# A last residual added by an identity product, and weight splits handed out two granules earlier, in a hybrid mLSTM and attention block

## The chip, the cores and the metric

The kernel runs on one NeuronCore of one Trainium2 chip. The metric is the device time of one execution in microseconds. The engines are TensorE (PE, with its weight loads shown as PEld), VectorE (DVE), ScalarE (ACT), GpSimd (POOL) and SyncE (SP, which issues the DMAs of weights and output). Each works through its own list of instructions in order and waits at semaphores for the others.

## The reference

The input x has 512 rows (tokens) of 1024 numbers, all in float32. One layer is computed:

- h = rmsnorm(x); one projection of h gives the inputs of two branches (mLSTM in chunks, forgetting attention) and two gates gm and gf of 1024 channels each.
- mix = sigmoid(gm) * (y_m @ w_br_mlstm) + sigmoid(gf) * (y_f @ w_br_fox), and x = x + mix @ w_out.
- x = x + (silu(h2 @ w_gate) * (h2 @ w_up)) @ w_down, with h2 = rmsnorm(x) and 2816 inner channels.
- The output is rmsnorm(x) with the gain norm_f_g: x * (mean(x * x) + 1e-6) ** -0.5 * gain, row by row.

The change touches two places: the gates gm and gf with the branch projections (the branch stage), and the last residual addition with the final norm (the tail).

## The kernel before

**Products in split float32.** To keep float32 accuracy each operand is held as a high part, rounded to fp32r, and a low part, the rest. One product is then three fp32r products on PE (`three`: high by high, high by low, low by high). Weights come from HBM in slots of 128x2048 numbers into two staging buffers. Each slot holds granules; for each granule ScalarE writes the high part (`split_hi`, L584), VectorE subtracts it from the staged weights for the low part (`split_lo`, L943). A ring of four buffers holds split granules. Semaphores: `hi_split`, `lo_split` and `used` count the granules split high, split low and worked through by PE. SyncE loads a slot when `lo_split` says that the slot two before it is done.

**The branch stage.** It has four rounds c = 0 to 3, two blocks of 128 output channels in each. The round's granules begin at `br_first` = 29, 35, 41 and 51. In rounds 0 and 1 they are four granules of gate weights and two of branch weights (33, 34 and 39, 40). In rounds 2 and 3 each pair of gate blocks is computed by a run of seven products in place of eight: `seven_slot` makes four granules of them (41 to 44 and 45 to 48 in round 2), two of which (42 and 43, the combos) are sums of weight quarters that VectorE computes first in `weight_sums` (L1337 to L1342, four instructions). The results are put together by VectorE's `run_sums` (L1299, steps 0 to 4, counted by `up_step`), after ScalarE has copied one piece to `parts` (`keep_first`, L772). The branch granules of round 2 are 49 and 50. After the branch products of a block VectorE makes the mix in three steps (L1388, L1390, L1393), ScalarE its high part (`mixT_hi`, L815), VectorE its low part (L1395).

PE's work on a run is `in_seven`: it takes four PSUM banks, (6, 4, 5, 7). `take(bank, by)` waits for the event that freed the bank last time and notes the one that frees it this time. It begins with

```
take(one, (kept, i + 1))
take(two, (up_step, UP_STEPS * i + 2))
pe.wait_ge(lo_split, g + 1)
```

`take_t_lo` (L1323) makes the low parts of token sums that the runs need; `token_sums` (L1319) makes the sums.

**Order of the splits.** ScalarE and VectorE walk the granules g in the same order as PE, and at each g first split the granules that `br_ahead(g)` names (`hi_ahead`, `lo_ahead`; the latter also does `weight_sums` when the granule begins a run), then do what g's own results ask. With AHEAD = 2, `br_ahead(g)` names g + 2 below 41, both 43 and 44 at 41, and g + 3 above.

**The second half of the down projection and the tail.** Output rows are four blocks r of 128 tokens. The down projection makes columns 0 to 511 in banks 4 to 7, then columns 512 to 1023 in banks 0 to 3. In this second half the last four granules (RING) are worked row block by row block, so that block 0 is done early. For each of the blocks 0 to 2 VectorE adds bank r to `x1` (L1518), ScalarE squares the sum and sums the squares (L561), VectorE makes the mean (L914), POOL its power -1/2 (L516, `rstd`), VectorE applies rstd and gain (L919), SyncE stores it. The last block goes in halves: VectorE multiplies the first half by the gain ahead of time (L1523), then after PE's last product adds the residual (L1525) and multiplies the second half by the gain (L1527); ScalarE squares the second half of x1 meanwhile. When rstd is there, VectorE scales the first half (L1531) and ScalarE the second (L905), each followed by its own DMA.

Of the kernel before, what the change touches and what calls it, by code (L numbers as in the profile page):

```python
# [17 lines left out]
ACT = mybir.ActivationFunctionType  # L18
ALU = mybir.AluOpType
# [3 lines left out]
D = 1024  # L23
SEQ = 512
ROWS = SEQ // P
KD = D // P
HALF = D // 2
# [28 lines left out]
AHEAD = 2  # L56
# [3 lines left out]
def block_kernel(nc, x, norm1_g, w_in, b_in, conv_w, conv_b, mlstm_norm_g, w_br_mlstm,  # L60
# [75 lines left out]
    br_first = []  # L136
# [8 lines left out]
    G_OUT = len(granules)  # L145
# [12 lines left out]
    D_GRAN = F_BLOCKS // 2  # L158
# [7 lines left out]
    N_GRAN = len(granules)  # L166

    ctx = ExitStack()
    with ctx:
# [3 lines left out]
        def at(name, shape, dtype, offset):  # L173
            return nc.alloc_sbuf_tensor_at(name, shape, dtype, offset=base + offset)
# [6 lines left out]
        x1 = at("x1", [P, ROWS, D], F32, A)  # L181
# [9 lines left out]
        gain_a = at("gain_a", [P, D], F32, G)  # L191
# [3 lines left out]
        work = [at(f"work{i}", [P, SEQ], F32, W + 2 * K * i) for i in range(6)]  # L195
        square_out = at("square_out", [P, D], F32, W + 8 * K)
# [42 lines left out]
        aT_lo = at("aT_lo", [P, F_BLOCKS, SEQ], F32R, R)  # L239
        aT_hi = at("aT_hi", [P, F_BLOCKS, SEQ], F32R, R + 44 * K)  # L240
# [16 lines left out]
        def small(name, shape, dtype=F32):  # L257
            n = int(np.prod(shape[1:])) * (2 if dtype == BF16 else 4)
            t = at(name, shape, dtype, small_at[0])
            small_at[0] += (n + 31) // 32 * 32  # L260
            assert base + small_at[0] <= nc.sbuf_usable_end, small_at[0]
            return t

        ident = small("ident", [P, P])
# [7 lines left out]
        square_sum = small("square_sum", [P, ROWS, 2])  # L272
# [19 lines left out]
        psum = [ctx.enter_context(nc.psum_tensor(f"bank{i}", [P, 512], F32)) for i in range(8)]  # L292

        def sem(name):
            return ctx.enter_context(nc.semaphore(name))
# [5 lines left out]
        gained, last_half = sem("gained"), sem("last_half")  # L301
# [3 lines left out]
        hi_split, lo_split, used = sem("hi_split"), sem("lo_split"), sem("granule_used")  # L305
        consts = sem("consts")
        vec_T, vec_ready = sem("vec_T"), sem("vec_ready")
        norm = [{n: sem(f"{n}_{i}") for n in ("squared", "summed", "rstd_ready", "xn_ready", "xn_T",
                                              "hT_hi_ready", "hT_lo_ready")} for i in range(3)]
# [21 lines left out]
        row_down, x2_ready, stored = sem("row_down"), sem("x2_ready"), sem("stored")  # L331
# [22 lines left out]
        def ring(tiles, g):  # L354
            n = granules_shape(g)
            return tiles[g % RING][:, :].rearrange("p (k c) -> p k c", k=n)
# [9 lines left out]

        def br_ahead(g):

            if g < br_first[2]:
                return [g + AHEAD]  # L370
            return [a for a in ([g + AHEAD] if g == br_first[2] else []) + [g + AHEAD + 1] if a < G_OUT + AHEAD]

        def run_banks(g):
            if g < G_FFN:
# [179 lines left out]
        def _(act):  # L554
            def square(i, src, r, halves):
                for half in halves:
                    n = count_squares[i]
                    if n:

                        act.wait_ge(norm[i]["squared"], n)  # L560
                    act.activation(square_out[:, 0:HALF], src[:, r, half * HALF:(half + 1) * HALF], ACT.Square,  # L561
                                   scale=D ** -0.5, accum_out=square_sum[:, r, half:half + 1]).then_inc(norm[i]["squared"], 1)
                    count_squares[i] += 1

            count_squares = [0, 0, 0]
# [8 lines left out]
            def split_hi(g):  # L574
                if g >= N_GRAN:
                    return
                if g in combos:
                    i, n = combos[g]
                    act.wait_ge(s_step, 4 * i + 2 + 2 * n)
                else:  # L580
                    wait_stage(act, g)
                if g >= RING:
                    act.wait_ge(used, g - RING + 1)
                act.activation(ring_part(w_hi, g), staged(g), ACT.Copy).then_inc(hi_split, 1)  # L584
# [189 lines left out]
            def hi_ahead(g):  # L774
                for a in br_ahead(g):
                    split_hi(a)
# [9 lines left out]
            for c in range(4):  # L786
                g = br_first[c]
# [60 lines left out]
            for p in range(F_BLOCKS // 2):  # L848
                g = ffn_first[p]
# [15 lines left out]
                g = ffn_up[p]  # L865
# [31 lines left out]
                        square(2, x1, r, (0,))  # L897
            for n in range(AHEAD):
                split_hi(N_GRAN - AHEAD + n)
            for r in range(ROWS):  # L900
                act.wait_ge(x2_ready, ROWS + r + 1)
                square(2, x1, r, (1,))
            act.wait_ge(gained, 2)
            act.wait_ge(norm[2]["rstd_ready"], ROWS)
            act.activation(x1[:, ROWS - 1, HALF:D], work[1][:, :], ACT.Copy,  # L905
                           scale=rstd[:, ROWS - 1:ROWS]).then_inc(last_half, 1)
# [3 lines left out]
        def _(dve):  # L910
            def mean_of_squares(i, r, n_squares):

                dve.wait_ge(norm[i]["squared"], n_squares)
                dve.scalar_tensor_tensor(out=mean_sq[:, r:r + 1], in0=square_sum[:, r, 0:1], scalar=EPS,  # L914
                                         in1=square_sum[:, r, 1:2], op0=ALU.add, op1=ALU.add).then_inc(norm[i]["summed"], 1)
# [428 lines left out]
            def lo_ahead(g):  # L1344
                for a in br_ahead(g):
                    split_lo(a)
                    if a in runs:
                        weight_sums(a)

            for c in range(4):  # L1350
                g = br_first[c]
# [96 lines left out]
            for p in range(F_BLOCKS // 2):  # L1448
                last = p == F_BLOCKS // 2 - 1
                g = ffn_first[p]  # L1450
# [20 lines left out]
                g = ffn_up[p]  # L1471
# [50 lines left out]
            r = ROWS - 1  # L1522
            dve.tensor_tensor(work[0][:, :], x1[:, r, 0:HALF], gain_a[:, 0:HALF], ALU.mult).then_inc(gained, 1)  # L1523
            dve.wait_ge(used, N_GRAN)
            dve.tensor_tensor(x1[:, r, HALF:D], x1[:, r, HALF:D], psum[r][:, :], ALU.add).then_inc(x2_ready, 1)  # L1525
            dve.wait_ge(x2_ready, 2 * ROWS)
            dve.tensor_tensor(work[1][:, :], x1[:, r, HALF:D], gain_a[:, HALF:D], ALU.mult).then_inc(gained, 1)  # L1527
            mean_of_squares(2, r, ROWS + r + 1)
            dve.wait_ge(norm[2]["rstd_ready"], r + 1)
            dve.wait_ge(gained, 1)  # L1530
            dve.tensor_scalar(x1[:, r, 0:HALF], work[0][:, :], rstd[:, r:r + 1], None, ALU.mult).then_inc(norm[2]["xn_ready"], 1)  # L1531
# [3 lines left out]
        def _(pe):  # L1535
            freed = {}

            def take(bank, by):

                if bank in freed:  # L1540
                    pe.wait_ge(*freed[bank])
                freed[bank] = by

            def three(o, a_hi, a_lo, b_hi, b_lo, first, last):

                pe.matmul(o, a_hi, b_hi, start=first, stop=False)  # L1546
                pe.matmul(o, a_hi, b_lo, start=False, stop=False)  # L1547
                return pe.matmul(o, a_lo, b_hi, start=False, stop=last)  # L1548
# [72 lines left out]
            def row_product(g, bank, r, src_hi, src_lo, k0, first, last):  # L1621

                wh, wl = ring(w_hi, g), ring(w_lo, g)
                rows = slice(r * P, (r + 1) * P)
                for k in range(2):
                    ins = three(psum[bank][:, :], src_hi[:, k0 + k, rows], src_lo[:, k0 + k, rows], wh[:, k, :], wl[:, k, :],
                                first and k == 0, last and k == 1)
                return ins
# [31 lines left out]
            for g, b in qk_block.items():  # L1660
# [4 lines left out]
                if b == 1:  # L1665
# [3 lines left out]
                    for j in range(ROWS):  # L1669
                        last = pe.transpose(psum[1][:, 16 * j:16 * j + 16], gate_rows[0:16, j * P:(j + 1) * P], ident[0:16, 0:16])  # L1670
# [32 lines left out]
            for n, g0 in enumerate((G_MV, G_FV)):  # L1703
                for d in range(4):
                    pe.wait_ge(lo_split, g0 + d + 1)
                    for r in range(ROWS):
                        if d == 0:
                            take(V_BANKS[n][r], (v_ready, ROWS * n + r + 1))
                        last = row_product(g0 + d, V_BANKS[n][r], r, hT_hi, hT_lo, 2 * d, d == 0, d == 3)
# [193 lines left out]
            for c in range(4):  # L1903
# [10 lines left out]
                for j in range(2):  # L1914
                    g, b = g0 + 4 + j, 2 * c + j
# [9 lines left out]
            for d in range(4):  # L1925
                pe.wait_ge(lo_split, G_OUT + d + 1)
                pe.wait_ge(mix_lo_ready, 2 * d + 2)
                for r in range(ROWS):
                    last = row_product(G_OUT + d, 4 + r, r, mixT_hi, mixT_lo, 2 * d, d == 0, d == 3)
                last.then_inc(used, 1)  # L1930
            one = transpose_halves(xn2)
            for r in range(ROWS):
                take(r, (x1_ready, ROWS + r + 1))
                for d in range(4):
                    if r == 0:
                        pe.wait_ge(lo_split, G_OUT + 4 + d + 1)
                    last = row_product(G_OUT + 4 + d, r, r, mixT_hi, mixT_lo, 2 * d, d == 0, d == 3)
# [30 lines left out]
            for half in range(2):  # L1968
                bank0 = 4 - 4 * half
                for r in range(ROWS):  # L1970
                    take(bank0 + r, (x2_ready, ROWS * half + r + 1))
                n_shared = D_GRAN - half * RING
                for d in range(n_shared):
                    g = G_DOWN + half * D_GRAN + d
                    pe.wait_ge(lo_split, g + 1)
                    pe.wait_ge(aT_lo_ready, 2 * d + 2)
                    for r in range(ROWS):
                        last = row_product(g, bank0 + r, r, aT_hi, aT_lo, 2 * d, d == 0, d == D_GRAN - 1)
                    last.then_inc(used, 1)
            for r in range(ROWS):  # L1980
                for d in range(D_GRAN - RING, D_GRAN):
                    g = G_DOWN + D_GRAN + d
                    if r == 0:
                        pe.wait_ge(lo_split, g + 1)
                    last = row_product(g, r, r, aT_hi, aT_lo, 2 * d, False, d == D_GRAN - 1)
# [91 lines left out]
```

## Time and profile before

| what | us |
|---|---|
| runs (3): median, lowest, highest | 761.53, 761.28, 761.60 |
| the profiled execution: its own time | 761.63 |
| its span, first to last instruction | 759.9 |
| PE matmuls busy in it | 747.3 |
| DVE busy | 529.3 |
| ACT busy | 312.4 |
| POOL busy | 24.1 |
| mean granted clock of TensorE, share of 2.4 GHz | 0.997 |

The page's times are of one execution that the hardware profiler recorded. The span lacks what lies around the first and the last instruction, so it is shorter than the execution's own time. Busy time of PE holds the latency of pipelined products: a product's duration (0.28 us for 256 columns) is longer than the distance to the next start. An idle time in brackets is the engine's, before that instruction, with the instruction that ended it.

### The profile page before, as it was taken

The numbers are of one execution on the slowest core, as the hardware profiler recorded it, in microseconds if no ns is written. First come the engines' busy times: TensorE is split into PE (matmuls) and PEld (weight loads), VectorE is DVE, ScalarE is ACT, GpSimd is POOL, SyncE is SP. The second block draws the span as 40 slices with busy tenths as digits, with TensorE's granted clock in tenths as the row PEclk, the third lists the DMA queues.
The fourth block names the chain that finished last, engine by engine and source line by source line (L and its number), as shares of the span: only waits on it lengthen the run. The fifth ranks groups of instructions, "written<-read, shape, count | busy, mean of one in ns | idle before, by whom it ended". The sixth has DMA issues, their size and how long they took to land.

```text
span 759.9 us, 11767 instructions
## 1 busy us (share of the span) xinstructions
PE 747.3 (98%) x4755; PEld 655.7 (86%) x4755; DVE 529.3 (70%) x806; ACT 312.4 (41%) x492; POOL 24.1 (3%) x51
## 2 busy tenths in 40 slices
PE   8999999999999999999999999999999999999996
PEld 7988888888676788899888999999999998888885
DVE  5878734347988587986356799999999998533123
ACT  5553213344555343443335344444444445433111
POOL 4000000011200000000000000000000000000000
PEclk9999999999999999999999999999999999999999
DMA  8533323301111031516511313333332334321302
GB/s 244 146 111 111 111 67 127 111 1 56 57 57 57 15 97 56 166 57 212 201 59 56 111 56 112 111 113 111 105 86 93 106 112 166 111 100 66 111 0 111
DMA packets 61802, 75.25 MB, mean 99 GB/s; under 512 B 3682, under 2 KB 49842, under 8 KB 61748
## 3 DMA queue, kind: packets, MB, share of 16 engines
q1 hardware_dynamic: 61744, 74.50, 30.5%
q8 instruction: 38, 0.62, 0.3%
q14 instruction: 16, 0.13, 0.1%
q10 hardware_dynamic: 4, 0.00, 0.0%
HBM read 72.40 MB, written 2.10 MB: 98 GB/s over the span
## 4 chain that ended last, share of the span: by engine, by line
PE 69%; DVE 2%; issue 1%; ACT 1%; POOLq 0%; POOL 0%; ACTq 0%; DVEq 0%
PE bank L1546 22%; PE bank L1548 21%; PE bank L1547 21%; PE bank L1809 1%; PE bank L1771 1%; PE bank L1792 1%; DVE w_lo L943 1%; ACT w_hi L584 0%; DVE t_lo L1323 0%; PE bank L1778 0%; PE bank L1559 0%; DVE t_sum L1319 0%; PE bank L1775 0%; DVE mix_sum L1393 0%; DVE mix_sum L1388 0%
## 5 line engine op out<-in xcount | busy, mean ns | idle before, releaser
L943 DVE TENSOR_TENSOR w_lo<-stage,w_hi 128x1024 fp32r<-128x1024 f32 (+1 forms) x125 | 139.1, 1122 | 114.3 <-ACT w_hi L584 105.3
L1546 PE MATMUL bank<-hT_hi,w_hi 128*128 128x256 f32 (+1 forms) x588 | 193.9, 330 | 0.7 <-issue 0.4
L1548 PE MATMUL bank<-hT_hi,w_lo 128*128 128x256 f32 (+1 forms) x588 | 191.2, 325 | 0.0
L1547 PE MATMUL bank<-hT_lo,w_hi 128*128 128x256 f32 (+1 forms) x588 | 191.1, 325 | 0.0
L584 ACT ACTIVATE w_hi<-stage 128x1024 fp32r<-128x1024 f32 x126 | 122.9, 977 | 143.1 <-PE bank L1548 134.5
L1546 PEld LDWEIGHTS bank<-hT_hi,w_hi 128*128 128x128 f32 x588 | 111.9, 190 | 9.9 <-issue 1.1
L1548 PEld LDWEIGHTS bank<-hT_hi,w_lo 128*128 128x128 f32 x588 | 111.8, 190 | 9.3
L1547 PEld LDWEIGHTS bank<-hT_lo,w_hi 128*128 128x128 f32 x588 | 111.9, 190 | 8.2
L1546 PE MATMUL bank<-t_hi,w_hi 128*128 128x256 f32 x368 | 104.4, 284 | 2.0 <-DVE w_lo L943 2.0
L1547 PE MATMUL bank<-t_lo,w_hi 128*128 128x256 f32 x368 | 104.1, 283 | 0.0
L1548 PE MATMUL bank<-t_hi,w_lo 128*128 128x256 f32 x368 | 104.1, 283 | 0.0
L584 ACT ACTIVATE w_hi<-s_sum 128x1024 fp32r<-128x1024 f32 x46 | 48.8, 1060 | 70.3 <-DVE s_sum L1339 55.9
L1546 PEld LDWEIGHTS bank<-t_hi,w_hi 128*128 128x128 f32 x368 | 70.6, 192 | 2.4 <-DVE w_lo L943 2.4
L1547 PEld LDWEIGHTS bank<-t_lo,w_hi 128*128 128x128 f32 x368 | 70.7, 192 | 0.0
L1548 PEld LDWEIGHTS bank<-t_hi,w_lo 128*128 128x128 f32 x368 | 70.6, 192 | 0.0
L1546 PE MATMUL bank<-w_hi,aT_hi 128*128 128x512 f32 x176 | 68.5, 389 | 0.0
L1547 PE MATMUL bank<-w_lo,aT_hi 128*128 128x512 f32 x176 | 68.5, 389 | 0.0
L1548 PE MATMUL bank<-w_hi,aT_lo 128*128 128x512 f32 x176 | 68.5, 389 | 0.0
L943 DVE TENSOR_TENSOR w_lo<-s_sum,w_hi 128x1024 fp32r<-128x1024 f32 x46 | 55.9, 1216 | 0.8 <-ACT w_hi L584 0.8
L1548 PEld LDWEIGHTS bank<-w_hi,aT_lo 128*128 128x128 f32 x176 | 33.0, 188 | 6.9
L1547 PEld LDWEIGHTS bank<-w_lo,aT_hi 128*128 128x128 f32 x176 | 33.0, 188 | 6.9
L1546 PEld LDWEIGHTS bank<-w_hi,aT_hi 128*128 128x128 f32 x176 | 33.0, 188 | 6.7
(218 smaller groups left out, 1052.4 us busy)
## 6 DMA issues: line engine op xcount, KB each, us to landing
stage<-in_w_in SPq DMA_DIRECT2D x21, 1024.0 KB, 5.2
stage<-in_w_gate SPq DMA_DIRECT2D x11, 1024.0 KB, 5.3
stage<-in_w_up SPq DMA_DIRECT2D x11, 1024.0 KB, 5.3
stage<-in_w_down SPq DMA_DIRECT2D x22, 512.0 KB, 4.5
stage<-in_w_out SPq DMA_DIRECT2D x4, 1024.0 KB, 8.9
x_nat<-in_x SPq DMA_DIRECT2D x4, 512.0 KB, 5.7
stage<-in_w_br_mlstm SPq DMA_DIRECT2D x4, 512.0 KB, 3.4
stage<-in_w_br_fox SPq DMA_DIRECT2D x4, 512.0 KB, 4.5
```

The lines of the kernel that those rows point to most:

```text
L584: act.activation(ring_part(w_hi, g), staged(g), ACT.Copy).then_inc(hi_split, 1)
L943: dve.tensor_tensor(ring_part(w_lo, g), staged(g), ring_part(w_hi, g).bitcast(F32), ALU.subtract).then_inc(lo_split, 1)
L1546: pe.matmul(o, a_hi, b_hi, start=first, stop=False)
L1547: pe.matmul(o, a_hi, b_lo, start=False, stop=False)
L1548: return pe.matmul(o, a_lo, b_hi, start=False, stop=last)
L1771: pe.matmul(banks[h2][:, 0:n], q_f[head, hp, q * P:(q + 1) * P], k_f[head, hp, 0:n], start=True, stop=False)
L1792: ins = pe.transpose(psum[2 + low][:, c:c + HALF_ARRAY], probs[u % 4][half, j * P:(j + 1) * P], ident[half, half])
L1809: last = pe.matmul(psum[FOX_Y][h2 * DH_F:(h2 + 1) * DH_F, q * P:(q + 1) * P], v_f[:, j, c:c + DH_F], pT[:, h2, j * P:(j + 1) * P], start=( ...
```

## The change

Three edits:

- `br_ahead` changes over two granules earlier: it names g + 2 below 39, both 41 and 42 at 39, and g + 3 above. So 42 is split at 39 and not at 40, 43 at 40 and not at 41, and everything from 44 on where it was.
- PE begins the second half of the down projection with a product of the identity matrix and the second half of the last row block of x1, in full float32, into bank 3. It starts that bank's accumulation; the first weight product of that block adds to it.
- In the tail of the last block the residual addition is left out. ScalarE squares bank 3 directly once PE's last granule is done. VectorE makes the mean first, then multiplies bank 3 by the gain into `work[1]`.

```diff
-            if g < br_first[2]:
+            if g < br_first[2] - 2:
                 return [g + AHEAD]
-            return [a for a in ([g + AHEAD] if g == br_first[2] else []) + [g + AHEAD + 1] if a < G_OUT + AHEAD]
+            return [a for a in ([g + AHEAD] if g == br_first[2] - 2 else []) + [g + AHEAD + 1] if a < G_OUT + AHEAD]
...
-            for r in range(ROWS):
+            for r in range(ROWS - 1):
                 act.wait_ge(x2_ready, ROWS + r + 1)
                 square(2, x1, r, (1,))
+            act.wait_ge(used, N_GRAN)
+            act.wait_ge(norm[2]["squared"], count_squares[2])
+            act.activation(square_out[:, 0:HALF], psum[ROWS - 1][:, :], ACT.Square, scale=D ** -0.5,
+                           accum_out=square_sum[:, ROWS - 1, 1:2]).then_inc(norm[2]["squared"], 1)
...
             dve.wait_ge(used, N_GRAN)
-            dve.tensor_tensor(x1[:, r, HALF:D], x1[:, r, HALF:D], psum[r][:, :], ALU.add).then_inc(x2_ready, 1)
-            dve.wait_ge(x2_ready, 2 * ROWS)
-            dve.tensor_tensor(work[1][:, :], x1[:, r, HALF:D], gain_a[:, HALF:D], ALU.mult).then_inc(gained, 1)
             mean_of_squares(2, r, ROWS + r + 1)
+            dve.tensor_tensor(work[1][:, :], psum[r][:, :], gain_a[:, HALF:D], ALU.mult).then_inc(gained, 1)
             dve.wait_ge(norm[2]["rstd_ready"], r + 1)
...
+                if half:
+
+                    pe.matmul(psum[ROWS - 1][:, :], ident[:, :], x1[:, ROWS - 1, HALF:D], start=True, stop=False)
...
-                        last = row_product(g, bank0 + r, r, aT_hi, aT_lo, 2 * d, d == 0, d == D_GRAN - 1)
+                        last = row_product(g, bank0 + r, r, aT_hi, aT_lo, 2 * d, d == 0 and not (half and r == ROWS - 1),
+                                           d == D_GRAN - 1)
```

## Rows read from the trace of the kernel before

**Rows 1.** The page, busy us, share of the span, instructions of each engine.

```profile
PE 747.3 (98%) x4755; PEld 655.7 (86%) x4755; DVE 529.3 (70%) x806; ACT 312.4 (41%) x492; POOL 24.1 (3%) x51
```

**Rows 2.** Waits of PE: waiter, waited for, us in total, times, longest.

```profile
PE bank L1546 <- DVE w_lo L943: 2.0, 2, 1.7
```

**Rows 3.** Timeline of PE, 299 to 311 us: start, us, instruction, idle before.

```profile
300.09 0.39 PE L1546 MATMUL bank<-t_hi,w_hi 128*128 128x256 f32 x1 [0.29 <-DVE w_lo L943]
...
302.95 0.28 PE L1548 MATMUL bank<-t_hi,w_lo 128*128 128x256 f32 x1
304.94 0.39 PE L1546 MATMUL bank<-t_hi,w_hi 128*128 128x256 f32 x1 [1.72 <-DVE w_lo L943]
305.16 0.28 PE L1547 MATMUL bank<-t_lo,w_hi 128*128 128x256 f32 x1
...
309.92 0.35 PE L1546 MATMUL bank<-hT_hi,w_hi 128*128 128x256 f32 x1 [0.40 <-issue]
```

**Rows 4.** Timeline of DVE, 295 to 310 us.

```profile
295.09 0.68 DVE L1388 SCALAR_TENSOR_TENSOR mix_sum<-work,bank 128x512 f32<-128x512 f32 x1
...
298.81 1.23 DVE L943 TENSOR_TENSOR w_lo<-s_sum,w_hi 128x1024 fp32r<-128x1024 f32 x1 [0.26 <-ACT w_hi L584]
299.95 0.68 DVE L1388 SCALAR_TENSOR_TENSOR mix_sum<-work,bank 128x512 f32<-128x512 f32 x1
...
302.71 0.69 DVE L1395 SCALAR_TENSOR_TENSOR mixT_lo<-mix_sum,mixT_hi 128x512 fp32r<-128x512 f32 x1 [0.76 <-ACT mixT_hi L815]
303.66 1.23 DVE L943 TENSOR_TENSOR w_lo<-s_sum,w_hi 128x1024 fp32r<-128x1024 f32 x1 [0.26 <-ACT w_hi L584]
304.80 1.82 DVE L943 TENSOR_TENSOR w_lo<-stage,w_hi 128x512 fp32r<-128x512 f32 x2
...
309.41 0.41 DVE L1299 TENSOR_TENSOR parts<-bank,parts 128x256 f32<-128x256 f32 x1
```

**Rows 5.** Timeline of ACT, 302 to 305 us.

```profile
302.05 0.63 ACT L815 ACTIVATE mixT_hi<-mix_sum 128x512 fp32r<-128x512 f32 x1 [3.27 <-DVE mix_sum L1393]
...
303.53 0.61 ACT L584 ACTIVATE w_hi<-stage 128x512 fp32r<-128x512 f32 x1
304.05 0.36 ACT L772 ACTIVATE parts<-bank 128x256 f32<-128x256 f32 x1
304.31 1.05 ACT L584 ACTIVATE w_hi<-stage 128x1024 fp32r<-128x1024 f32 x1
```

**Rows 6.** Timeline of all engines in the tail, 753 to 757 us.

```profile
753.35 0.39 PE L1547 MATMUL bank<-w_lo,aT_hi 128*128 128x512 f32 x1
...
753.57 0.39 PE L1548 MATMUL bank<-w_hi,aT_lo 128*128 128x512 f32 x1
754.00 0.69 DVE L1525 TENSOR_TENSOR x<-x,bank 128x512 f32<-128x512 f32 x1 [1.26 <-PE bank L1548]
754.72 0.63 ACT L561 ACTIVATE square_out<-x 128x512 f32<-128x512 f32 x1 [4.71 <-DVE x L1525]
...
755.48 0.16 DVE L914 SCALAR_TENSOR_TENSOR mean_sq<-square_sum 128x1 f32<-128x1 f32 x1
755.72 0.54 POOL L516 TENSOR_TENSOR rstd<-mean_sq,minus_half 128x1 f32<-128x1 f32 x1 [4.90 <-DVE mean_sq L914]
...
756.35 0.72 ACT L905 ACTIVATE x<-work,rstd 128x512 f32<-128x512 f32 x1 [0.91 <-POOL rstd L516]
```

**Rows 7.** Timeline of PE near the start, two float32 products and what follows.

```profile
4.72 1.13 PE L1640 MATMUL bank<-gain_row,ones 1*128 1x512 f32 x4 [0.74 <-DMA gain_row<-in_norm_g]
5.78 0.71 PE L1634 MATMUL bank<-ones 128*128 128x128 f32 x4
```

**Rows 8.** Groups of ACT by shape: busy us, mean ns of one, idle before.

```profile
L836 ACT ACTIVATE y_pair<-bank 128x512 f32<-128x512 f32 x4 | 2.4, 598 | 7.1 <-PE bank L1548 6.2 <-DVE aT L1428 0.9
```

**Rows 9.** Windows: us, busy of PE, PEld, DVE, ACT, POOL, granted clock, DMA, GB/s.

```profile
5.00:10.00 5.00, 3.78 (x19) 2.86 (x18) 3.19 (x5) 3.08 (x6) 2.26 (x10) 0.76 1.13 338
10.00:15.00 5.00, 4.67 (x35) 4.41 (x34) 3.41 (x5) 4.37 (x8) 2.78 (x3) 0.90 0.84 198
...
302.00:304.00 2.00, 1.23 (x11) 1.02 (x9) 1.03 (x2) 1.95 (x3) 0.00 (x0) 1.00 0.00 0
```

## The prediction, made before the change was run

> **What bounds the kernel now.** I read the engine shares first: TensorE's matmuls are busy 98% of the span [rows 1], so what delays PE in mid-kernel delays the end, and only what follows PE's last product can be shortened without it. Then the waits of PE: its largest is 2.0 us in 2 waits for VectorE's `w_lo`, the longest 1.7 [rows 2]. The timeline puts both in round c = 2 of the branch stage, in the first run of seven products (granules 41 to 44; br_first is 29, 35, 41, 51). Products there start 0.12 us apart. PE waits ahead of granule 42 (0.29), ahead of 43 (1.72) and a third time, 0.40, ahead of granule 45, which the views call issue [rows 3]. A restart costs more than its bracket: from 302.95 to 304.94 is 1.99 where 0.12 would do, and the next start is 0.22 later and not 0.12, together 1.97 lost. In the same way the first costs 0.55 and the third 0.64: 3.16 us in the three.
>
> The third is what matters. `in_seven(45)` begins with `take(one)` and `take(two)`, and bank 4 (two) is free once `up_step` is 2: that is `run_sums(41, 1)`, the second of the two L1299 additions, which ends at 309.41 + 0.41 = 309.82, just ahead of PE's 309.92 [rows 3, 4]. So the end of this stretch is set by VectorE's queue: what stands before that addition there, and the gaps in it.
>
> The last view is the tail: PE's last product is over at 753.57 + 0.39 = 753.96, then come the residual addition (DVE L1525), the squares (ACT L561), their mean, the rstd on POOL, and ACT's L905 at 756.35 [rows 6]. The output's DMAs follow.
>
> **Part 1, the splits.** `br_ahead` now hands out two granules at 39 and not at 41. Old: at 39 split 41, at 40 split 42, at 41 split 43 and 44, at 42 split 45. New: at 39 split 41 and 42, at 40 split 43, at 41 split 44, at 42 split 45, and the same from there. No instruction is added. On VectorE `split_lo(42)` passes in front of `take_t_lo(3)` and the first mix, `split_lo(43)` in front of the second mix. One split takes 1.14 us of its queue (298.81 to 299.95) [rows 4].
>
> New VectorE order: split 42 starts when the first weight sums are issued, 1.14 ahead of the first mix's old slot less the `take_t_lo` (1.14 too): about 293.95. ScalarE's half can be done by then, since it needs only the first two sums and no mix. The first mix starts at 295.09 + 1.14 = 296.23, split 43 at 298.81 + 1.14 = 299.95 (it still stands behind the mix's round trip to ScalarE, as split 42 did), done 301.18; the second mix at 301.09, its last step at 302.71 + 1.14 = 303.85, over at 304.54 [rows 4]. PE then has no wait at 42 (it gets there at 300.09 - 0.29 - 0.28 + 0.12 = 299.64), none at 43 (24 products later, 302.52), and it comes to 44 at 305.40, whose low half (0.6 us from 304.54) is ready about 305.2. So those waits really go, and PE has done granule 44's 12 products at 306.84.
>
> And there it meets the bank. VectorE has still split 44, split 45, four weight sums of granule 45 and two run sums to do, the same instructions as before. Its gaps: both mixes keep their round trips. Of the wait for split 43's high half at the end (302.71 + 0.69 = 303.40 to 303.66, about 0.26) nothing is left, since split 44's high half is only 512 wide. But split 45 now waits: ScalarE's chain hangs on the second mix, its `mixT_hi` going from 302.05 to 303.19; split 44 follows at 303.72, `parts` at 304.24 (0.52 later, as 303.53 to 304.05), split 45 at 304.50 (0.26 later), over at 305.55 [rows 5]. Before, VectorE began split 45 0.59 into the pair of 304.80, at about 305.39; now it can at 305.59 [rows 4]. So `run_sums(41, 1)` ends at 310.02 and PE starts granule 45 at about 310.12. **The splits cost 0.2 us**: three waits of 3.16 us become one of about 3.2 (306.90 to 310.12). Bounds: -0.3 (split 45 in time and the 0.26 gap gone) to +0.6 (another round trip of 0.4 shows). SyncE's loads hang on `lo_split`: the slot of 49 and 50 waits for 44, which is done at 305.2 and not 305.4, so no load comes later. The wait for `mix_step` in later rounds has a round's length (10 us or more) of room. After 45 PE waits nowhere for VectorE in this stage [rows 2], so a lateness of 0.2 goes straight to the end.
>
> **Part 2, the identity product.** PE gets one product of full float32, 128x128 by 512 columns, at the start of the second half of the down projection, where it works without a pause. It stands on PE's path in full; its operand has been in SBUF since the first residual. Each float32 product that is no transpose leaves two records. The nearest row: two such products with 512 columns side by side in different rows of the array, four records, take 5.78 - 4.72 = 1.06 us until the next product starts [rows 7]. The fp32r products of the down projection lie 0.22 apart [rows 6], so two records at that pace, 0.45 us, are the lower bound; 1.3 (the 1.06 and one more product's pace) is the upper. I take 1.0, near the 1.06 with something off for the start of that row after a wait.
>
> **Part 3, the tail.** L1525 goes: `act.wait_ge(used)` lets ScalarE square from the bank itself. Before, L1525 started at 754.00 and the square at 754.72, so 0.72 goes. ScalarE may wake some hundredths later than VectorE did; against that, ScalarE's 512-wide operation with constant scale took 598 ns out of a bank and the square 630 out of SBUF [rows 6, 8]. From PE's end: square 754.05, its sum over 754.77 (0.73 later, as 754.72 to 755.45), mean 754.80 to 754.96, rstd 755.04 to 755.58. The gain product of the second half now stands behind the mean on VectorE and reads the bank: 754.95 to 755.64 at 0.69 us. Before, it lay beside the square; now it lies beside the rstd (0.54) and is 0.06 longer. L905 waits for both: 755.67. **The tail gives 0.68 us** (756.35 - 755.67). The first half's L1531 stands behind the product and starts at about 755.62, also some 0.67 earlier. Bounds: 0.5 (the bank read costs both engines 0.1 more) to 0.78.
>
> **Sum.** +0.20 (splits) + 1.00 (identity) - 0.68 (tail) = +0.52. Profiled execution: span 759.90 to 760.42, and with the 1.73 around it (761.63 - 759.90) 762.15. The median of the runs is 0.10 below the profiled one, so 762.05: **762.0 us**, 0.07% over 761.53. The ends of the terms: -0.3 + 0.45 - 0.78 = -0.6 and 0.6 + 1.3 - 0.5 = +1.4, so the likeliest case reaches from 760.9 to 762.9. A measurement of this kernel tells about 0.2%, 1.5 us, from no change; the likeliest case lies inside that.
>
> **Rivals.**
> *A, the clock falls in the joined wait.* PE now stands still 3.2 us in one piece where it stood 1.7 at most. With a wait of that length the granted clock stayed 1.00 (302 to 304) [rows 9]; but near the start, where PE was busy 3.78 of 5 us in short pieces with waits between, it went down to the 1.2 GHz level: means of 0.76 and 0.90 in two stretches of 5 us are (0.24 + 0.10) x 5 / 0.5 = 3.4 us at the low level [rows 9]. If that comes after 310, products of 256 columns (0.12 us each at 2.4 GHz, 0.21 at 1.2) lose about 3.4 x (1 - 0.12 / 0.21) = 1.5 us of work, and PE has no slack to make it up. Then 762.0 + 1.5 = 763.5, slower than before. It decides if the idle piece that costs the clock lies somewhere between 1.7 and 3.2 us; what speaks against it is only that nothing fell around the old wait of 1.7. 30%.
> The Trainium skill, page TensorE: Matmul & The Clock Gate, section Why this matters for your kernels, warns of long idle gaps between bursts of products since the clock falls back after one. No row here shows a gap of this length in mid-kernel; by that rule the sum would be that of rival A, without it that of the forecast.
>
> *B, the joined wait is shorter.* If bank 4 were not what holds granule 45 (the view calls that wait issue, and does not name L1299), all 3.16 us go: 759.90 - 3.16 + 0.32 in the span, 758.7 us. For it: the views name only `w_lo`. Against it: PE starts 0.1 after the addition ends, and the code waits for it. A half-way case, VectorE freed of a round trip or two (0.76 to 1.5 us), would give 760.5 to 761.3. Together 12%, of which the full 758.7 has 6%.
>
> *C, the identity product is cheap.* At 0.45 us the sum is -0.03: 761.5. It needs two float32 records at the fp32r pace, against the 1.06 us. 8%; it is inside the likeliest case's range.
>
> **How the numbers follow.** Forecast 50%, A 30%, B 12%, C 8%. Range 760.9 to 763.8: from the low end of the likeliest case, past A; it leaves out B in the main. Faster by over 0.2% needs most of B: 7%. Slower by over 0.2% (above 763.05) is A and a little of the forecast's upper end: 31%. Within: 62%.
>
> **What would show it.** Right: no wait of PE at granules 42 and 43; one of about 3 us ahead of the first product of 45, ending just after L1299's second addition, at 310.1; two records of the new product of ident and x1 ahead of the second half, about 1.0 us from the first of them to the next fp32r product; ACT's square 0.1 after PE's last product; L905 1.7 us after PE's end and not 2.4. The clock 1.00 at 310 to 316 against 0.50 tells the forecast from A. Wrong: granule 45 starting before 309, or the product's records 0.22 apart.

## The result, and the profile after

| | us |
|---|---|
| before, 9 runs: median, lowest, highest | 761.60, 761.28, 761.94 |
| after, 9 runs: median, lowest, highest | 763.72, 762.17, 764.88 |
| ratio, 95% interval | 1.0026, 1.0016 to 1.0036 |
| profiled execution after: its own time, its span | 763.72, 762.0 |

The kernel became slower by 2.1 us, inside the stated range, but at the time of rival A (763.5) and not at the forecast's (762.0). The nine runs lie in three bunches: three at 762.2 to 762.4, three at 763.5 to 763.7 and three at 764.7 to 764.9. The top three lie above the range's end, 763.8, and the median 0.08 us under it: the range held because it was drawn past rival A. The profiled execution is one of the middle bunch. The nine runs of before in the table lie within 0.7 us; in the later runs of the same kernel a second bunch about 1 us higher appears (see e2), so beside the median of all 77 runs of before, 761.84, the change costs 1.9 us. Line numbers of the new kernel are a little higher: L1303 is the old L1299 (run_sums), L1548 to L1550 the old L1546 to L1548, L909 the old L905, and L905 the new square.

The waits of PE after (waiter, waited for, total us, times, longest), to be held beside [rows 2]:

```profile
PE bank L1548 <- DVE parts L1303: 3.1, 1, 3.1
```

Timeline of PE and VectorE after, to be held beside [rows 3, 4]:

```profile
300.35 1.23 DVE L947 TENSOR_TENSOR w_lo<-s_sum,w_hi 128x1024 fp32r<-128x1024 f32 x1 [0.26 <-ACT w_hi L584]
...
304.86 0.69 DVE L947 TENSOR_TENSOR w_lo<-stage,w_hi 128x512 fp32r<-128x512 f32 x1
305.99 1.23 DVE L947 TENSOR_TENSOR w_lo<-stage,w_hi 128x1024 fp32r<-128x1024 f32 x1 [0.44 <-ACT w_hi L584]
...
310.00 0.41 DVE L1303 TENSOR_TENSOR parts<-bank,parts 128x256 f32<-128x256 f32 x1
```

```profile
307.11 0.28 PE L1550 MATMUL bank<-t_hi,w_lo 128*128 128x256 f32 x1
310.52 0.55 PE L1548 MATMUL bank<-hT_hi,w_hi 128*128 128x256 f32 x1 [3.12 <-DVE parts L1303]
310.87 0.41 PE L1549 MATMUL bank<-hT_lo,w_hi 128*128 128x256 f32 x1
311.08 0.41 PE L1550 MATMUL bank<-hT_hi,w_lo 128*128 128x256 f32 x1
...
313.40 0.28 PE L1549 MATMUL bank<-hT_lo,w_hi 128*128 128x256 f32 x1
```

The waits at 42 and 43 are gone. One wait of 3.12 us stands ahead of granule 45, and this time the view names VectorE's `run_sums` as what ended it. All of this is 0.4 us later than forecast because the whole execution is (see below); the distances are as forecast. The pair 310.52 to 310.87 to 311.08 shows the second thing: products of 256 columns 0.21 us apart. The windows (columns as in [rows 9]) show the granted clock:

```profile
308.00:310.00 2.00, 0.00 (x0) 0.00 (x0) 2.00 (x4) 1.27 (x2) 0.00 (x0) 0.98 0.97 334
310.00:312.00 2.00, 1.48 (x7) 1.51 (x8) 2.00 (x4) 1.36 (x2) 0.00 (x0) 0.50 0.00 0
312.00:314.00 2.00, 2.00 (x14) 2.00 (x14) 1.97 (x4) 0.77 (x2) 0.00 (x0) 0.67 0.03 8
314.00:316.00 2.00, 2.00 (x19) 2.00 (x18) 0.93 (x2) 1.67 (x3) 0.00 (x0) 1.00 0.02 2
```

It fell to the 1.2 GHz level at about 309.92, 0.6 us before the wait's end, and stayed there for (0.02 + 0.50 + 0.33) x 2 / 0.5 = 3.4 us. Of that the last 2.8 us had products. What the Trainium skill says of long idle gaps (TensorE: Matmul & The Clock Gate, Why this matters for your kernels) thus holds in this trace.

The identity product, and the tail beside [rows 6]:

```profile
695.57 0.39 PE L1550 MATMUL bank<-w_hi,aT_lo 128*128 128x512 f32 x1
695.80 1.02 PE L1976 MATMUL bank<-x,ident 128*128 128x512 f32 x2
696.26 0.80 PE L1548 MATMUL bank<-w_hi,aT_hi 128*128 128x512 f32 x1
696.89 0.40 PE L1549 MATMUL bank<-w_lo,aT_hi 128*128 128x512 f32 x1
...
756.32 0.39 PE L1550 MATMUL bank<-w_hi,aT_lo 128*128 128x512 f32 x1
756.75 0.60 ACT L905 ACTIVATE square_out<-bank 128x512 f32<-128x512 f32 x1 [3.99 <-PE bank L1550]
...
757.54 0.16 DVE L918 SCALAR_TENSOR_TENSOR mean_sq<-square_sum 128x1 f32<-128x1 f32 x1 [2.05 <-ACT square_out L905]
757.61 0.69 DVE L1530 TENSOR_TENSOR work<-bank,gain_a 128x512 f32<-128x512 f32 x1
757.77 0.54 POOL L516 TENSOR_TENSOR rstd<-mean_sq,minus_half 128x1 f32<-128x1 f32 x1 [4.21 <-DVE mean_sq L918]
758.35 0.49 DVE L1533 TENSOR_SCALAR x<-work,rstd 128x512 f32<-128x512 f32 x1
758.41 0.72 ACT L909 ACTIVATE x<-work,rstd 128x512 f32<-128x512 f32 x1 [0.98 <-POOL rstd L516]
```

Without L1976 the product L1548 would start at 695.80 and L1549 0.227 later, at 696.02; L1549 starts at 696.89. So the identity product costs 0.87. The tail from PE's end (756.32 + 0.39 = 756.71) to the last scaling (758.41) is 1.70, and was 2.39.

The start: this execution met the low clock there in another way than the one before.

```profile
12.15 0.55 PE L1548 MATMUL bank<-hT_hi,w_hi 128*128 128x256 f32 x1
12.50 0.42 PE L1549 MATMUL bank<-hT_lo,w_hi 128*128 128x256 f32 x1
...
13.08 0.28 PE L1549 MATMUL bank<-hT_lo,w_hi 128*128 128x256 f32 x1
```

The first weight products still run 0.2 us apart until 12.9. The 25th weight product starts at 15.46 us here and at 15.11 in the trace before, so 0.35 us were lost by then, ahead of everything that the change touches. VectorE's split of granule 43 was forecast for 299.95 and stands at 300.35: 0.40 us.

The difference of the two spans, 2.1 us, is then: start 0.40 + splits 0.20 + low clock 1.24 (the product of 313.40, the fourteenth, would have started at 310.52 + 0.20 + 12 x 0.12 = 312.16) + identity product 0.87 - tail 0.69 = 2.02. The spans are given to 0.1 us, so nothing of size is left over.

### The profile page after: what moved, and what is told of

The parts are those of the page before. It is cut to its first block, busy times and chain, and to the rows that moved or that the text cites. A ratio compares the mean times of both kernels' runs of the same rounds, so it can differ in the third digit from the quotient of the medians.

```text
span 762.0 us, 11771 instructions
## 1 busy us (share of the span) xinstructions
PE 750.9 (99%) x4757; PEld 658.5 (86%) x4757; DVE 528.7 (69%) x805; ACT 312.7 (41%) x492; POOL 24.1 (3%) x51
## 4 chain that ended last, share of the span: by engine, by line
PE 68%; DVE 3%; issue 2%; ACT 1%; POOLq 0%; POOL 0%; ACTq 0%; DVEq 0%
PE bank L1548 21%; PE bank L1549 21%; PE bank L1550 21%; PE bank L1811 1%; PE bank L1773 1%; PE bank L1794 1%; ACT w_hi L584 0%; DVE w_lo L947 0%; DVE t_lo L1327 0%; PE bank L1780 0%; PE bank L1561 0%; DVE t_sum L1323 0%; PE bank L1777 0%; DVE mix_sum L1397 0%; DVE s_sum L1343 0%
## 5 line engine op out<-in xcount | busy, mean ns | idle before, releaser
L1548 PE MATMUL bank<-hT_hi,w_hi 128*128 128x256 f32 (+1 forms) x588 | 194.7, 331 | 3.1 <-DVE parts L1303 3.1
L1550 PE MATMUL bank<-hT_hi,w_lo 128*128 128x256 f32 (+1 forms) x588 | 191.8, 326 | 0.0
L1549 PE MATMUL bank<-hT_lo,w_hi 128*128 128x256 f32 (+1 forms) x588 | 191.8, 326 | 0.0
L1548 PEld LDWEIGHTS bank<-hT_hi,w_hi 128*128 128x128 f32 x588 | 112.7, 192 | 12.0 <-issue 3.3
L1550 PEld LDWEIGHTS bank<-hT_hi,w_lo 128*128 128x128 f32 x588 | 112.5, 191 | 9.3
L1549 PEld LDWEIGHTS bank<-hT_lo,w_hi 128*128 128x128 f32 x588 | 112.7, 192 | 8.3
L1548 PE MATMUL bank<-t_hi,w_hi 128*128 128x256 f32 x368 | 104.1, 283 | 0.0
L1549 PE MATMUL bank<-t_lo,w_hi 128*128 128x256 f32 x368 | 104.1, 283 | 0.0
L1550 PE MATMUL bank<-t_hi,w_lo 128*128 128x256 f32 x368 | 104.1, 283 | 0.0
L1548 PEld LDWEIGHTS bank<-t_hi,w_hi 128*128 128x128 f32 x368 | 70.7, 192 | 0.0
L1549 PEld LDWEIGHTS bank<-t_lo,w_hi 128*128 128x128 f32 x368 | 70.7, 192 | 0.0
L1550 PEld LDWEIGHTS bank<-t_hi,w_lo 128*128 128x128 f32 x368 | 70.7, 192 | 0.0
L1548 PE MATMUL bank<-w_hi,aT_hi 128*128 128x512 f32 x176 | 68.9, 391 | 0.0
L1549 PE MATMUL bank<-w_lo,aT_hi 128*128 128x512 f32 x176 | 68.5, 389 | 0.0
L1550 PE MATMUL bank<-w_hi,aT_lo 128*128 128x512 f32 x176 | 68.5, 389 | 0.0
L1548 PEld LDWEIGHTS bank<-w_hi,aT_hi 128*128 128x128 f32 x176 | 33.0, 188 | 7.1 <-issue 0.2
L1549 PEld LDWEIGHTS bank<-w_lo,aT_hi 128*128 128x128 f32 x176 | 33.0, 188 | 7.0 <-issue 0.2
L1550 PEld LDWEIGHTS bank<-w_hi,aT_lo 128*128 128x128 f32 x176 | 33.0, 188 | 6.8
```

## The experiments

Each ran beside runs of the kernel before, whose median was 761.97 beside e1 to e4 (35 runs), 761.99 beside e5 to e8 (22 runs) and 761.57 beside e9 to e11 (11 runs). Times are medians with lowest and highest in brackets; the ratio to before is given with its 95% interval. Every kernel has its own line numbers: L1548 to L1550, L1553 to L1555, L1561 to L1563 and L1573 to L1575 are the same three products, L1303 and L1309 are `run_sums`.

### The change taken apart

**e1_splits_only**

```diff
-            if g < br_first[2]:
+            if g < br_first[2] - 2:
...
-            return [a for a in ([g + AHEAD] if g == br_first[2] else []) + [g + AHEAD + 1] if a < G_OUT + AHEAD]
+            return [a for a in ([g + AHEAD] if g == br_first[2] - 2 else []) + [g + AHEAD + 1] if a < G_OUT + AHEAD]
```

> Edit: of the change only the earlier splits (br_ahead); the tail and the down projection as before. Theory (joined wait and clock): PE's three waits of round 2 become one of 3.1 us ahead of granule 45, and the clock falls to the low level behind it in most executions, which costs about 1.2 us beside the 0.2 us of VectorE's queue. So the times lie in two groups, about 761.8 and 763.1, with most in the upper one, and the spread of the runs is over 1 us. Rival (the excess over the forecast comes from the identity product or the tail): all runs near 761.8, spread as before, 0.6 us.

Measured: 763.44 (761.60 to 764.72, 12 runs) against 761.97 (761.28 to 762.95, 35 runs); 1.0018 (1.0010 to 1.0027). Two of the twelve are at 761.6, seven at 762.9 to 763.7, three at 764.6 to 764.7. Wait and clock:

```profile
PE bank L1546 <- DVE parts L1299: 3.1, 1, 3.1
```

```profile
308.00:310.00 2.00, 0.00 (x0) 0.00 (x0) 2.00 (x5) 1.35 (x2) 0.00 (x0) 1.00 0.95 329
310.00:312.00 2.00, 1.56 (x12) 1.59 (x13) 2.00 (x4) 1.29 (x2) 0.00 (x0) 0.96 0.00 0
312.00:314.00 2.00, 2.00 (x11) 2.00 (x11) 1.97 (x4) 0.84 (x2) 0.00 (x0) 0.50 0.04 8
314.00:316.00 2.00, 2.00 (x14) 2.00 (x14) 0.86 (x2) 1.69 (x3) 0.00 (x0) 0.69 0.02 3
```

The split edit alone gives the slow median and the spread. Here the fall came 1.4 us after PE had started again (at 310.44), so the low level met products all the way, where in the changed kernel's trace it came 0.6 us before PE's restart: when it comes differs from execution to execution. A third bunch near 764.7 had not been expected, and no trace shows one. It lies as far above the middle bunch as one more piece at the low level would cost (1.2 us), and in the changed kernel's nine runs the three highest have a mean granted clock of 0.993, 0.993 and 0.996, the middle three 0.997. But the mean does not count the low level near the start in every execution (see the last section), and in e1 a middle run (763.65) has 0.994 as well as the top ones, so the cause of this bunch stays open.

**e2_product_and_tail**: the changed kernel with the old `br_ahead`.

> Edit: of the change only the identity product and the new tail; the splits as before. Theory: no long wait of PE, no fall of the clock in mid-kernel; +0.88 (the product, as the profile after has it) - 0.69 (tail) = +0.2, so about 761.8 with the narrow spread of before. Rival (the excess comes from here): about 763.3, with the wide spread of the changed kernel.

Measured: 762.01 (761.69 to 763.10, 11 runs), ratio 1.0001 (0.9993 to 1.0010). The rival is out: product and tail do not carry the 2 us. The spread was not as narrow as I wrote, and the profile, of an execution of the upper bunch (762.97), says why:

```profile
302.00:304.00 2.00, 1.43 (x12) 1.23 (x11) 0.98 (x3) 1.74 (x3) 0.00 (x0) 1.00 0.00 0
304.00:306.00 2.00, 0.84 (x4) 0.84 (x5) 2.00 (x3) 1.58 (x3) 0.00 (x0) 0.83 0.00 0
306.00:308.00 2.00, 2.00 (x12) 2.00 (x11) 1.97 (x3) 0.00 (x0) 0.00 (x0) 0.50 0.60 144
308.00:310.00 2.00, 2.00 (x16) 2.00 (x16) 2.00 (x6) 1.18 (x2) 0.00 (x0) 0.82 1.08 375
```

With the old waits (2.0 us in two, as before) the clock fell in this execution too. The PE rows price it:

```profile
305.16 0.46 PE L1548 MATMUL bank<-t_hi,w_hi 128*128 128x256 f32 x1 [1.73 <-DVE w_lo L947]
...
311.06 0.28 PE L1548 MATMUL bank<-hT_hi,w_hi 128*128 128x256 f32 x1
```

From the restart at granule 43 to the first product of granule 45 it took 5.90 us, and 4.98 in the trace before (304.94 to 309.92 [rows 3]). The fall costs 0.92 us there, less than in the changed kernel, since the old short wait ahead of 45 is swallowed by it. The kernel before has the same two bunches: 27 of its 77 runs are at 762.15 or more (none of the 9 beside the changed kernel, 16 of 35 beside e1 to e4, 10 of 22 beside e5 to e8, 1 of 11 beside e9 to e11), the others at 762.00 or less, and the medians of the bunches, 762.60 and 761.63, are 1.0 apart. That each run of the upper bunch had such a fall is argued from this distance; the trace of e2 shows one. So the old waits cost the clock in a part of the executions, and the joined wait makes it the rule.

**e3_tail_alone**: e2 without the product; the residual of the last block's second half is left out.

> Edit: splits as before, the new tail, and no identity product: the second half of the last row block goes without its residual, which the reference has. Theory: the tail alone takes 0.69 us off, so 760.9; against the kernel with product and tail the difference is the product's cost, 0.88. Rival (the product is hidden in the shadow of something else in the down projection): the same time as with the product, about 761.8, or with it, 760.9 for both.

Measured: 761.58 (760.82 to 762.04, 11 runs), ratio 0.9994 (0.9986 to 1.0003). The median is 0.7 above what I wrote, by its two bunches probably for the same reason as in e2: five runs are at 760.8 to 761.05, and the profiled one of them (761.05) shows no fall. The lowest of e3 and e2 are 0.87 apart, as the product in the trace; the medians only 0.43. The sign is clear, the size rests on the trace.

### Is it the idle wait that costs the clock?

**e4_filled_wait**

```diff
                 take(one, (kept, i + 1))
+                if i == 1:
+                    for _ in range(12):
+                        pe.matmul(psum[one][:, :], hT_hi[:, 0, 0:P], hT_hi[:, 1, :], start=True, stop=True)
                 take(two, (up_step, UP_STEPS * i + 2))
```

> Edit: the changed kernel, with twelve fp32r products of 512 columns (2.7 us, operands of hT_hi, into bank 6, whose next product overwrites them) put between take(one) and take(two) of in_seven(45), that is into PE's wait of 3.1 us. The wait's end is VectorE's, so it does not move. Theory (an idle piece of that length costs the clock): no fall of the clock behind granule 45, all runs in the lower group, about 762.0, with a spread under 1 us, 1.2 us or more under the median of the changed kernel. Rival (the slow runs of the changed kernel are something else, as a phase of the launch or the product near 696): the median stays at 763.7 with the same spread. If the filler itself delays PE the time is higher by what the profile shows between 310 and 311.

Measured: 762.12 (761.92 to 762.91, 11 runs), ratio 1.0002 (0.9993 to 1.0011). Ten of eleven runs lie in 0.45 us.

```profile
306.87 2.91 PE L1888 MATMUL bank<-hT_hi 128*128 128x512 f32 x12
310.12 0.39 PE L1548 MATMUL bank<-hT_hi,w_hi 128*128 128x256 f32 x1 [0.34 <-DVE parts L1303]
310.35 0.28 PE L1549 MATMUL bank<-hT_lo,w_hi 128*128 128x256 f32 x1
```

Granule 45 starts at 310.12, as forecast, and its products are 0.12 apart; the windows from 306 to 314 have a granted clock of 1.00. Twelve products whose results nobody reads take 1.6 us off the changed kernel (and 1.3 off e1, which ran beside it and carries the same wait). So the excess is the clock's, and the clock went because PE stood idle. It also gives the forecast its own measurement: 762.05 predicted without a fall, 762.12 measured.

### What holds granule 45?

**e7_sums_ahead**: in the first run of round 2 VectorE adds before it splits.

```diff
                         lo_ahead(g)
-                        lo_ahead(g + 1)
-                        run_sums(g, 0)
-                        run_sums(g, 1)
+                        if c == 2 and k == 0:
+                            run_sums(g, 0)
+                            run_sums(g, 1)
+                            lo_ahead(g + 1)
+                        else:
+                            lo_ahead(g + 1)
+                            run_sums(g, 0)
+                            run_sums(g, 1)
```

> Edit: the changed kernel, with run_sums(41, 0) and (41, 1) on VectorE moved ahead of the split of 45 and the weight sums of 45. Theory: bank 4 is free at about 306.0, so the wait at 45 for it goes; but the split of 45 and the sums come 0.75 us later, so PE waits about 0.3 us at 45 and 1 us at 46 for the low halves. Together 1.3 us in place of 3.1, and too short for the clock to fall in most runs: about 760.3. Rival (it is the splits, not the bank, that hold 45): the wait stays near 3 us and the runs spread as in the changed kernel, 763.5.

Measured: 760.91 (760.53 to 761.24, 11 runs), ratio 0.9987 (0.9978 to 0.9996). Of the wait at 45 only 0.26 us is left (products at 306.72 and 307.10), near the 0.3 expected; the rival is out. What is late at 46 was misjudged: not its low half but the next bank, which waits for `run_sums(41, 3)`, 1.63 us, with the restart 1.80. The clock is 1.00 in this execution from 12 us to the end, and the runs lie within 0.7 us:

```profile
311.84 0.36 PE L1553 MATMUL bank<-t_hi,w_hi 128*128 128x256 f32 x1 [1.63 <-DVE br_quarters L1303]
```

**e5_late_mix**: the second mix of round 1 goes behind the first run of round 2, on both engines.

```diff
+                        if c == 2 and k == 0:
+                            take_mixT_hi(3)          
...
                         lo_ahead(g + 3)
+                        if c == 2 and k == 0:
+                            mix(1, 1, br_first[1] + 4)
...
-                    dve.wait_ge(used, g + j + 1)
...
+                    if b != 3:
+                        mix(c, j, g)
```

The new helpers `mix` and `take_mixT_hi` hold the code that stood in the loop; both engines leave out block 3 in its old place.

> Edit: the changed kernel, with the mix of block 3 (VectorE's four instructions and ScalarE's mixT_hi, the second mix of round 1) moved behind the first run of round 2, behind the split of granule 47. That takes 3.4 us of work and round trips out from ahead of run_sums(41, 1). Theory (that queue sets the start of granule 45): run_sums(41, 1) ends about 306.6, PE comes to 45 at 306.8, the wait goes from 3.1 us to under 0.3 and with it the fall of the clock; 762.0 - 3.2 = 758.8, all runs within 1 us. Rival (VectorE is the bound over the whole round, 87% busy): the work comes back as waits of PE at 46 to 50, and the gain against the changed kernel's lower group is under 1 us, so 761 or more.

Measured: 760.07 (759.75 to 760.25, 9 runs), ratio 0.9973 (0.9964 to 0.9983). The spread is 0.5 us, and the clock column of this trace stays at 1.00. `run_sums(41, 1)` ends at 306.07, and the view lists no wait of PE in round 2. I had forecast 758.8: a wait came back in round 3, at granule 55, the same place of the next round, 1.14 us with its restart.

```profile
337.82 0.28 PE L1563 MATMUL bank<-t_hi,w_lo 128*128 128x256 f32 x1
339.08 0.36 PE L1561 MATMUL bank<-hT_hi,w_hi 128*128 128x256 f32 x1 [0.98 <-issue]
```

```profile
338.56 0.41 DVE L1309 TENSOR_TENSOR parts<-bank,parts 128x256 f32<-128x256 f32 x1
```

The traces before and after have no wait there; in them PE comes 3 us later or more. The rival was right that work comes back, wrong in where and how much.

**e9_both_mixes_late**: the same with the second mix of round 2 and round 3.

> Edit: e5, with the second mix of round 2 (block 5) moved behind the first run of round 3 in the same way. In e5 the wait came back as 1.0 us at granule 55, the first of the second run of round 3, whose bank 4 waits for run_sums(51, 1) (338.56 to 338.97, PE at 339.08). Theory: that mix stands in the same queue in the same place, so with it out of the way the last wait of the stage goes, 1.1 us with its restart: 759.0. Rival (VectorE's total work over rounds 2 and 3 is the bound by now): the wait moves to a later granule and the time stays within 0.3 us of e5, 760.

Measured: 758.89 (758.34 to 759.12, 5 runs), ratio 0.9965 (0.9952 to 0.9979), near the 759.0 expected; the rival is out. From 255 us, ahead of round 2, to the end the view lists no wait of PE.

**e11_both_late_old_splits**: e9 with the old `br_ahead`.

> Edit: e9 with the old br_ahead (43 and 44 split at 41). Theory: once the bank no longer holds PE, the earlier splits have their worth: split 42 stands behind the first mix and its round trip again, so PE waits at 42 for some 0.5 us with the restart, and little after that since the second mix is out of the way: 0.5 us over e9, 759.5. Rival (the earlier splits are worth nothing in any order): as e9.

Measured: 759.29 (759.07 to 759.59, 7 runs), ratio 0.9969 (0.9959 to 0.9980). A wait is back at 42:

```profile
PE bank L1561 <- DVE w_lo L953: 0.3, 1, 0.3
```

So the earlier splits are worth about 0.4 us once the bank is out of the way. The ranges of e9 and e11 overlap by 0.05 us, with few runs each.

### The product and the tail, without the clock's noise

**e8_late_mix_old_tail**: e5 with the old tail and no identity product.

> Edit: the kernel before with the earlier splits and the late mix of e5, but the old tail and no identity product. With no long wait there is no fall of the clock to blur it, so e5 less this is what the identity product and the tail bring together. Theory: +0.88 - 0.69 = +0.2, so this one at 758.6 and e5 at 758.8. Rival (product and tail gain on balance): this one slower than e5.

Measured: 759.93 (759.53 to 760.24, 7 runs), ratio 0.9972 (0.9962 to 0.9983). That is as far above its forecast as e5 is, and for the same reason: the wait at granule 55, 1.3 us here. e5 is 0.14 above it, where 0.2 was expected; the ranges overlap, so of the sign I am not sure, but a gain from product and tail together is not to be seen.

**e6_late_mix_split_product**: e5 with the residual split while the first half of the down projection runs, and

```diff
-
-                    pe.matmul(psum[ROWS - 1][:, :], ident[:, :], x1[:, ROWS - 1, HALF:D], start=True, stop=False)
+                    pe.wait_ge(resid_lo, 1)
+                    pe.matmul(psum[ROWS - 1][:, :], ident_r[:, :], x1_hi[:, :], start=True, stop=False)
+                    pe.matmul(psum[ROWS - 1][:, :], ident_r[:, :], x1_lo[:, :], start=False, stop=False)
```

> Edit: e5 with the identity product in fp32r: ScalarE and VectorE split the residual into a high and a low part during the first half of the down projection, where both have room, and PE adds identity by high and identity by low. Theory (a full float32 product takes PE 0.88 us, an fp32r one 0.23): two products at 0.23 in place of 0.88 give 0.42 less than e5, so 758.4. Rival (the identity product's cost is the switch of its kind, not its passes): same as e5.

Measured: 759.67 (759.42 to 760.10, 6 runs), ratio 0.9971 (0.9959 to 0.9983): 0.40 under e5, 0.42 expected (6 and 9 runs, whose ranges overlap), and 0.26 under e8, which has neither product nor new tail.

**e10_both_late_split_product**: e9 and e6 together.

> Edit: e9 with the fp32r identity product of e6. Theory: 0.4 us under e9, as e6 is under e5: 758.6. Rival: as e9.

Measured: 758.34 (758.10 to 758.68, 5 runs), ratio 0.9958 (0.9945 to 0.9970). It is 0.55 under e9, where 0.4 was expected; with five runs each the ranges overlap. By medians it is 3.2 us under the kernel before that ran beside it, and 5.4 under the changed one. Its products:

```profile
690.58 0.39 PE L1575 MATMUL bank<-w_hi,aT_lo 128*128 128x512 f32 x1
690.80 0.39 PE L2001 MATMUL bank<-x_hi,ident_r 128*128 128x512 f32 x1
691.03 0.39 PE L2002 MATMUL bank<-x_lo,ident_r 128*128 128x512 f32 x1
691.26 0.40 PE L1573 MATMUL bank<-w_hi,aT_hi 128*128 128x512 f32 x1
```

Two products, 0.46 us, where the float32 one takes 0.87. By these rows product and tail now pay: 0.46 - 0.69 = -0.23.

## Why the prediction was right or wrong, point by point

- **Three waits become one, and the bank holds granule 45: right.** The views before named `w_lo` for two waits and nothing for the third; reading `take(two)` in the code beside the end of L1299 gave the place. e7 and e5 show it from two sides.
- **The splits cost 0.2 us: right.** VectorE's `run_sums(41, 1)` ends at 310.41 less the 0.40 of the start, 310.01, against 310.02; the new gap ahead of split 45 is 0.44.
- **The identity product, 1.0 us: somewhat high.** 0.87. The row it was taken from, two products side by side at the start, took 1.06; what the rest of it was no run shows.
- **The tail, -0.68: right**, -0.69. From PE's end the square was due at 0.09, the mean at 0.84, the gain product at 0.99 and the last scaling at 1.71; they came at 0.04, 0.83, 0.90 and 1.70. The gain product did lie beside the rstd.
- **The likeliest case has no fall of the clock, 50% against 30%: wrong.** This is the step that failed. The sum without a fall was right to 0.1 us (e4), a little by luck, since the identity product was taken 0.13 too dear; but a fall is the rule: in e1, ten of twelve runs are 1.2 us or more above the lowest two. The price of rival A, 1.5 us, was near: 1.24 in the profiled execution, 1.6 between the medians of the changed kernel and e4. What I had put on the side of no fall, that nothing fell around the old 1.7 us wait, was one execution, and the row shown for it, 302 to 304, ends before the wait does (304.94), though the later windows of that trace are at 1.00 too. e2 shows that the same wait costs the clock in another execution. So the condition of rival A, an idle piece somewhere between 1.7 and 3.2 us, was too sharp: the same waits cost the clock in one execution and not in another. The median fell where rival A had put it, within the stated range; the top bunch is outside it and has no explanation.
- **Rivals B and C: no.** The bank held granule 45 (3.12 us), and the identity product took 0.87 us, not 0.45.
- **The start differs by 0.40 us between the two profiled executions**, which no step had.

## What to carry to other kernels

When a wait is taken away, ask for the next thing that the same instruction stream needs from the same late engine. Here the splits came earlier and the additions that free a bank did not, since they stand in the same queue: PE moved only when the additions came ahead of other work there (e7) or the mixes were taken out from ahead of them (e5, e9). Several short waits and one long one of the same sum are not equal on TensorE: here the long one cost its clock in ten of twelve runs of e1, the short ones, by the bunches, in 27 of 77 of before. One profile without a fall is no evidence that there is none. If a wait can't be removed, products that nobody reads can fill it; that only gives back the clock (e4 is no faster than the kernel before). And a residual added by PE pays only if it costs less than the addition it replaces at the end: split in two fp32r products it does, in full float32 it does not.

## What the runs showed of the hardware

- With an idle piece of 3.1 us the granted clock fell to 1.2 GHz for 3.4 us in both profiled executions (after, e1), 0.6 us before PE restarted in one and 1.4 us after it in the other; by their times it fell in most of the others too. With the old waits of 0.3 and 1.7 us it fell in one of three profiled executions (before, e2, e3). A single wait of 1.6 us (e7), 1.3 (e8) or 1.0 (e5) had no fall behind it in the one trace of each. Cost: 1.24 us in the trace after, where 2.8 us of it had products, and 0.92 in e2. Apart from the start, no trace shows the low level anywhere else.
- Near the start the windows give a granted clock of 1.00 until 12.9 us in the profile after, while products of 256 columns are 0.2 us apart. In the trace before, products at this place are 0.12 us apart, and the column shows 0.50 from 8 to 10 us. So here, ahead of the first change that the column shows, the distance of products tells the level and the column does not.
- A full float32 product of 128x128 by 512 columns leaves two records 0.46 us apart and costs 0.87 us, 3.8 times the 0.227 of an fp32r one. The Trainium skill (FP8 and Floating Point Precision, TensorE Precision Notes) has four passes for true float32, which agrees.
- ScalarE's square with a sum took 0.60 us out of a bank and 0.63 out of SBUF.
